# Two transformer blocks on one core: other banks for three folded norms, a shorter wait before their first passes, and edits at the head and in the convolution's tail

## Time and profile before

| | us |
|---|---|
| median of 3 runs | 1256.05 (1254.77 to 1258.88) |
| the profiled execution's own time | 1254.8 |
| its span in the trace | 1253.1 |
| PE busy in the span | 1216.1 (97%) |
| the chain that ended last, on PE | 80% |
| bytes read from HBM | 352.58 MB, 282 GB/s over the span |

### The profile page before, as it was taken

The page is one execution under the profiler, slowest core; times in us unless marked ns, Lnnn a source line. Parts: engine busy times, 40 slices in busy tenths (PEclk is TensorE's granted clock), DMA queues, the critical chain, the costliest instruction groups (busy, mean ns, idle before and its releaser), DMA issues.

```text
span 1253.1 us, 16148 instructions
## 1 busy us (share of the span) xinstructions
PE 1216.1 (97%) x6246; PEld 821.3 (66%) x6246; DVE 721.4 (58%) x1337; ACT 519.4 (41%) x903; POOL 48.1 (4%) x96
## 2 busy tenths in 40 slices
PE   9999999999999999999999999999999999999996
PEld 8997888887777778888877976634444334443332
DVE  5786877777758778777778988522222222222222
ACT  5554444444567654444456435422232222232222
POOL 0000000000000000000002800000000000000000
PEclk9999999999999999999999999999999999999998
DMA  8558777651631397766614486999999999999995
GB/s 294 198 217 298 269 269 268 246 190 68 228 135 31 110 364 268 269 252 239 229 57 147 149 277 261 358 421 404 427 428 431 427 429 429 428 427 431 428 426 206
DMA packets 121564, 358.07 MB, mean 286 GB/s; under 512 B 8890, under 2 KB 67955, under 8 KB 105106
## 3 DMA queue, kind: packets, MB, share of 16 engines
q1 hardware_dynamic: 114912, 331.85, 68.4%
q0 software_dynamic: 6336, 25.17, 5.1%
q10 hardware_dynamic: 242, 0.06, 0.0%
HBM read 352.58 MB, written 1.05 MB: 282 GB/s over the span
## 4 chain that ended last, share of the span: by engine, by line
PE 80%; DVE 7%; DMA 7%; ACT 3%; issue 1%; ACTq 0%; SPq 0%; DVEq 0%
PE ps L444 15%; PE ps L446 15%; PE ps L445 15%; PE ps L3084 14%; PE ps L3122 7%; DMA third_gate_up<-in_moe_w_up 5%; DMA second_expert<-in_moe_w_up 2%; DVE w_lo L418 2%; PE ps L3060 2%; PE ps L2503 1%; DVE xn L2600 1%; PE ps L3138 1%; PE ps L3067 1%; PE ps L3141 1%; PE ps L1039 1%
## 5 line engine op out<-in xcount | busy, mean ns | idle before, releaser
L413 ACT CAST w_hi<-dense_weights 128x1024 fp32r<-128x1024 f32 (+1 forms) x228 | 235.4, 1042 | 234.0 <-PE ps L446 194.5
L418 DVE TENSOR_TENSOR w_lo<-dense_weights,w_hi 128x1024 fp32r<-128x1024 f32 (+1 forms) x228 | 273.3, 1210 | 84.2 <-ACT w_hi L413 83.5
L444 PE MATMUL ps<-w_hi,xT_lo 128*128 128x512 f32 (+1 forms) x596 | 235.7, 395 | 4.4 <-DVE xT_lo L941 2.0
L446 PE MATMUL ps<-w_hi,xT_hi 128*128 128x512 f32 (+1 forms) x596 | 230.7, 387 | 0.0
L445 PE MATMUL ps<-w_lo,xT_hi 128*128 128x512 f32 (+1 forms) x596 | 230.3, 386 | 0.0
L444 PEld LDWEIGHTS ps<-w_hi,xT_lo 128*128 128x128 f32 x596 | 112.0, 188 | 32.0 <-issue 4.1
L446 PEld LDWEIGHTS ps<-w_hi,xT_hi 128*128 128x128 f32 x596 | 112.0, 188 | 23.3
L445 PEld LDWEIGHTS ps<-w_lo,xT_hi 128*128 128x128 f32 x596 | 112.1, 188 | 21.9 <-issue 0.2
L3268 DVE SCALAR_TENSOR_TENSOR cmask<-g_v,ps 128x256 f32<-128x256 f32 x32 | 13.5, 421 | 167.1 <-ACT g_v L3197 167.1
L3259 DVE TENSOR_TENSOR hnT<-ps,g_bc 128x512 f32<-128x512 f32 x32 | 22.1, 692 | 149.2 <-PE ps L3122 149.2
L3197 ACT ACTIVATE g_v<-ps 128x256 f32<-128x256 f32 x32 | 12.3, 384 | 206.7 <-PE ps L3084 206.7
(11 more groups left out here) (441 smaller groups left out, 1844.4 us busy)
## 6 DMA issues: line engine op xcount, KB each, us to landing
ada_w<-in_ada_w POOLq DMA_DIRECT2D x12, 2048.0 KB, 12.1
dense_weights<-in_w_gate SPq DMA_DIRECT2D x22, 1024.0 KB, 7.1
dense_weights<-in_w_up SPq DMA_DIRECT2D x22, 1024.0 KB, 9.4
dense_weights<-in_w_down SPq DMA_DIRECT2D x22, 1024.0 KB, 5.1
dense_weights<-in_moe_w_gate SPq DMA_DIRECT2D x10, 2048.0 KB, 21.6
second_expert<-in_moe_w_gate SPq DMA_DIRECT2D x9, 2048.0 KB, 20.4
second_expert<-in_moe_w_up SPq DMA_DIRECT2D x9, 2048.0 KB, 24.8
third_gate_up<-in_moe_w_up SPq DMA_DIRECT2D x9, 2048.0 KB, 27.2
```

The costliest lines, as they stand in the source:

```text
L413: act.copy(split_view(w_hi, name, i, j), piece(name, i, j)).then_inc(hi_ready, 1)
L418: dve.tensor_tensor(split_view(w_lo, name, i, j), piece(name, i, j), split_view(w_hi, name, i, j).bitcast(F32), ALU.subtract).then_inc(pie ...
L444: pe.matmul(out, left[1], right[0], start=start, stop=False)
L446: return pe.matmul(out, left[0], right[0], start=False, stop=stop)
```

## The change

1. **Norms.** Norms 1, 3 and 4 turn their chunks in banks 6, 7, 2, 3, in 4, 6, 5, 7 and in 4, 5, 2, 3. All folded norms do group 2 token tile by token tile. PE then waits for two finished chunks (four still in norms 2 and 5), and the piece loops behind norms 1, 3 and 4 wait for two more chunks before each piece.
2. **Head.** ACT issues one row load (`g_mix`), loads its table by a tiny activation, and issues the other 11 row loads later, behind the weight splits of the first block. The columns of `g_mix` are copied before the first split. The first 1 MB of weights comes in two DMAs; the warm-up counts are 12 and 14 for 24 and 6; the other columns of `cols_a` get a PE transpose and an ACT copy of their own in `pe_rest` and `act_rest`; `load_late` goes behind the loads of `ev_w_out`; the `dw_rows` load is cut in two. In the first piece PE waits for one high half, then for the second.
3. **Tail of the convolution.** `feature_cols` is copied by DVE, behind the first weighing; the weighing reads the gate from PSUM; the low part of the first block's last piece is made before the centring; the second block's first piece is split by ACT ahead of `act_rows`, which copies three banks for four.
4. **Experts' loads.** The gate half of expert 0 is issued after the taps on PE, expert 1's gate and up in four pairs of slices as the pieces of the second block are used, expert 2's up in two parts between them.

The diff, cut to its core (counts of landings that follow from it are left out):

```diff
@@ tokens_by_columns
-                    pe.wait_ge(*high)
-                    for part in range(2):
-                        for kk in range(2):
+                    for kk in range(2):
+                        pe.wait_ge(high[0], high[1] + kk * high[2])
+                        for part in range(2):
@@ columns (SP)
-                        sp.dma_start(dst[:, 0:4], wv[:, 0:4, c:c + n]).then_inc(gu_landed[0], 16)
+                        for piece_ in range(2):
+                            cut = slice(2 * piece_, 2 * piece_ + 2)
+                            sp.dma_start(dst[:, cut], wv[:, cut, c:c + n]).then_inc(gu_landed[piece_], 16)
...
-                    elif name == "ev_in" and i == 2:
-                        setup.load_late(sp)
@@ SP, behind the loads of ev_out
+            setup.load_late(sp)
@@ SP, experts
+            def feature_pair(e, k):
+                cut = slice(k, k + 2)
+                for side in range(2):
+                    sp.dma_start(gate_up_of(e)[:, side, cut], (g, u)[side][:, e, cut]).then_inc(gu_landed[e % TILES], 16)
...
             side_features(2, 0, 0, small_landed)
+            wait_split("conv_out", 0, 3, None)
+            gate_or_up(0, 0)
...
-            wait_split("conv_out", 0, 3, None)
-            gate_or_up(0, 0)
-            wait_split("conv_out", 1, 3, None)
-            side_features(0, 1, 1, gu_landed[0])
-            down_half(0, 0, down_landed[0])
+            for j in range(4):
+                if j == 1:
+                    wait_split("conv_out", 1, 3, None)
+                    side_features(0, 1, 1, gu_landed[0])
+                    down_half(0, 0, down_landed[0])
+                wait_used(sp, "conv_out", 1, j)
+                feature_pair(1, 2 * (PIECE_AT["conv_out", 1, j] % BUFFERS))
+                if j % 2 == 1:
+                    split_features(2, 1, j // 2)
             sp.wait_ge(h_ready, 28)
-            gate_up(1)
-            gate_or_up(2, 1)
@@ NormStage
-                banks = {0: (4, 5, 6, 7), 2: (4, 6, 5, 7), 5: (4, 6, 5, 7)}.get(self.index, (0, 1, 2, 3))
+                banks = {0: (4, 5, 6, 7), 1: (6, 7, 2, 3), 2: (4, 6, 5, 7), 3: (4, 6, 5, 7), 4: (4, 5, 2, 3),
+                         5: (4, 6, 5, 7)}.get(self.index, (0, 1, 2, 3))
...
-                    if self.folded and b % 2 == 0 and (self.index, b) != (3, 2):
-                        pe.wait_ge(h_ready, 4 * self.index - 2 + 2 * (b // 2))
-                    tiles_first = (self.index, b) == (3, 2)
+                    if self.folded and b == 0:
+                        pe.wait_ge(h_ready, 4 * self.index - 2)
+                    tiles_first = self.folded and b == 2
...
-                    pe.wait_ge(self.ready, KC * self.index + KC // 2)
+                    self.wait_chunk(pe, KC // 2 - 1 if self.index in (2, 5) else 1)
@@ FfnStage.pe
-                        if n == 0 and j == 2:
-                            self.norm.wait_rest(pe)
+                        if n == 0 and j >= 1:
+                            self.norm.wait_chunk(pe, 2 * j + 1)
@@ SetupStage
+            def load_table(self, act):
+                act.wait_ge(self.own_consts, 3)
+                act.activation(rtmp[:, 0, 0:1], ones[:, 0:1], ACT.Square)
...
-                warm_up(pe, 3, 24)
+                warm_up(pe, 3, 12)
                 pe.wait_ge(self.consts, 1)
-                pe.wait_ge(self.rows_landed, 16 * len(ROWS_A))
...
+                pe.wait_ge(gu_landed[2], 16)
...
-                warm_up(pe, 3, 6)
+                warm_up(pe, 3, 14)
@@ pe_rest
+                pe.wait_ge(self.rows_landed, 16 * (len(ROWS_A) - 1))
+                pe.transpose(ps[:, 6, ROWS_A_AT:ROWS_A_AT + N_ROWS_A], rows_a[0:N_ROWS_A, :], ident[0:N_ROWS_A, 0:N_ROWS_A])
@@ EvenStage.act
                 split_upto(act, split_hi, "ev_in", 0, 3)
+                setup.load_rows(act)
                 wait_used(act, "ev_in", 0, 3)
@@ OddIn.pe
-                        rest = lambda: self.norm.wait_rest(pe)
...
+                                      chunks=(self.norm.ready, KC * self.norm.index + 2, 2) if i == 0 else None)
@@ ConformerStage.act
-                mod.act_eights(act)
...
                 high(KC - 1)
+                split_upto(act, split_hi, "conv_out", 1, 0, ahead=0)
                 mod.act_rows(act)
@@ ConformerStage.dve
+                split_upto(dve, split_lo, "conv_out", 0, 3, ahead=0)
                 dve.wait_ge(self.conv, KC - len(CONV_PE))
...
+                    if c == 1:
+                        dve.wait_ge(mod.spread, 2)
+                        wait_a(dve, "conv_out", 1)
+                        weigh(0)
+                        mod.dve_eights(dve)
                     if 1 <= c <= KC:
                         finish(c - 1)
...
-                split_upto(dve, split_lo, "conv_out", 0, 3, ahead=0)
-                dve.wait_ge(mod.rows, 2)
-                wait_a(dve, "conv_out", 1)
```

More of the change, by code:

```diff
@@ L121 @@
 N_ROWS_A = sum(c for _, c in ROWS_A.values())
+FIRST_ROWS_A = ROWS_A["g_mix"][1]
 N_ROWS_B = sum(c for _, c in ROWS_B.values())
-SMALL_LANDED = 16 * (11 + len(ROWS_B))
-LATE_LANDED = 16 * 3
+ROWS_A_AT = 3 * P
+SMALL_LANDED = 16 * (12 + len(ROWS_B))
+LATE_LANDED = 16 * 4
 class Own:
@@ L532, in wait_gate_up @@
         def wait_gate_up(eng, e, it):
[L534 removed]
+            ahead = (16, LATE_LANDED + 96, 32)[e % TILES]
             eng.wait_ge(gu_landed[e % TILES], per_round(ahead + 32 * (e // TILES + 1), it, 32 * DOWN_TILES))
@@ L872, in act @@
                     if self.index == 0:
+                        gains(act)
                         split_upto(act, split_hi, *split_ahead, 0, ahead=0)
@@ L877, in act @@
                     act.activation(xn[:, 0], h[:, 0], ACT.Copy, scale=rstd[:, 0, 0:1]).then_inc(self.scaled, 1)
-                if gains is not None:
+                if gains is not None and self.index:
                     gains(act)
@@ L1267, in load_stream, with load_first_row @@
                     sp.dma_start(h[:, t], x[:, t]).then_inc(self.h_landed[t], 16)
+            def load_first_row(self, act):
+                for dst, src in list(self.rows(ROWS_A, rows_a))[:1]:
+                    act.dma_start(dst, src).then_inc(gu_landed[2], 16)
             def load_rows(self, act):
-                for dst, src in self.rows(ROWS_A, rows_a):
+                for dst, src in list(self.rows(ROWS_A, rows_a))[1:]:
                     act.dma_start(dst, src).then_inc(self.rows_landed, 16)
@@ L1396, in pe @@
                     tokens_by_columns(pe, "ev_in", i, (2 * i, 2 * i + 1), chunks=(norms[0].ready, 2, 2) if i == 0 else None,
-                                      high=(norms[0].hi, 2) if i == 0 else None)
+                                      high=(norms[0].hi, 1, 1) if i == 0 else None)
                 setup.pe_rest(pe)
@@ L1556, in pe @@
                         self.up.q_products(pe)
-                    tokens_by_columns(pe, "od_in", i, [2 * i + t for t in range(T)], width("od_in", i), rest, rest_at=3 if i == 2 else 2)
+                    tokens_by_columns(pe, "od_in", i, [2 * i + t for t in range(T)], width("od_in", i), rest, rest_at=3,
+                                      chunks=(self.norm.ready, KC * self.norm.index + 2, 2) if i == 0 else None)
             GATE_BANKS = (2, 5)
@@ L2285, in pe @@
                         tokens_by_columns(pe, "od_out", i, (4 + 2 * i, 5 + 2 * i), pieces=(2 * half, 2 * half + 1),
-                                          chunks=(self.lo, 3, 1) if late else None, high=(self.hi, 3) if late else None)
+                                          chunks=(self.lo, 3, 1) if late else None, high=(self.hi, 3, 0) if late else None)
                     if half == 0:
@@ L2394, in pe_eights, with dve_eights @@
                 last.then_inc(self.spread, 1)
-            def act_eights(self, act):
-                act.wait_ge(self.spread, 3)
-                act.copy(feature_cols[:], ps[:, 2, 0:2 * KC].rearrange("p (v k) -> p v k", v=2)).then_inc(self.rows, 1)
+            def dve_eights(self, dve):
+                dve.wait_ge(self.spread, 3)
+                dve.tensor_copy(feature_cols[:], ps[:, 2, 0:2 * KC].rearrange("p (v k) -> p v k", v=2)).then_inc(self.rows, 1)
             ROW_BANKS = (0, 1, 4, 5)
@@ L2410, in act_rows @@
                 act.wait_ge(self.spread, 2)
-                for i in range(2):
-                    bank = self.ROW_BANKS[2 * i]
-                    last = act.copy(g_bc[:, i].rearrange("p (j n) -> p j n", j=2), ps[:, bank:bank + 2, :])
-                last.then_inc(self.rows, 1)
+                act.copy(g_bc[:, 0, 0:512], ps[:, self.ROW_BANKS[0], :])
+                bank = self.ROW_BANKS[2]
+                act.copy(g_bc[:, 1].rearrange("p (j n) -> p j n", j=2), ps[:, bank:bank + 2, :]).then_inc(self.rows, 1)
         class ConformerStage:
@@ L2529, in pe @@
                     tokens_by_columns(pe, "conv_out", i, self.OUT_BANKS[i], chunks=(self.lo, 2, 2) if i == 0 else None,
```

(9 more changed lines are left out.)

33 lines of the change are left out of this document (18 added, 15 removed).

## The result

| | before | after |
|---|---|---|
| median | 1255.41 us (6 runs, 1254.31 to 1258.88) | 1246.89 us (6 runs, 1246.22 to 1251.70) |
| ratio, with its 95% interval | | 0.9933 [0.9915, 0.9951] |
| profiled execution's own time, span | 1254.8, 1253.1 | 1248.71, 1246.9 |

The change is faster by 0.7%.

The account below looks back on a forecast made before the run. PE was taken to set the pace up to 806 us, then the DMA engines by the experts' bytes. Head -0.95, norms -2.37, tail -1.93 and experts 0 made -5.25, from 1256.05 to 1250.8 us, range 1247.0 to 1254.8.

Parts of the forecast that it names:

- the head's term: Head: -0.95 us, from -1.5 for an earlier first transpose, +0.2 for one more transpose and +0.35 for a stall.
- The tail's term: Convolution's tail: -1.93 us, -0.88 from earlier tanh and -1.05 from the removed wait for `w_lo`; bounds -1.0 and -2.1.
- the base: Starting time from which the forecast subtracts its terms: 1256.05 us, the median of the runs before.
- The gain of -1.5: Head: PE's first transpose at 10.55 instead of 12.05 us; bounds -2.0 (PE at the rate of scaling) and +1.0.
- The stall of 0.35 at piece 7: Head: ACT's 11 late issues delay `gm_v` and `w_lo` of piece 7, so PE stalls +0.35 us (0 to 0.7).
- The extra transpose: Head: one more PE transpose of 121 rows, for the other columns, costs +0.2 us (0.1 to 0.3).
- Cover is that PE has no hole from 12.05 to 36.10: Head: reason for pricing the moved `load_late` at zero, ahead of weights that PE doesn't wait for.
- Norms, -2.37: Norms 1, 3 and 4: PE starts two chunks earlier, 3 x 0.79 us; bounds 0 and -3 x 1.0.
- The finer wait on high halves gives nothing: Convolution's tail: all chunks come 0.88 us earlier and so does the block's end; the finer wait adds zero.
- Experts and prefetch, 0: Experts' stream: 0 us, an unbroken stream replaced by a start-up of some 1.5 us; bounds -0.8 and +0.5.
- the same work: Routing, 787.7 to 804 us: work unchanged by the change, so no term in the sum.
- Rival 1: Routing: PE's half clock falls at another moment, about 1.0 us more gain, 1249.8 (1249.0 with experts' -0.8); chance 0.17.

Follow-up runs that it names:

- head alone: The kernel before with only the head's part of the change; 1252.64 us, ratio 0.9980.
- no prefetch: The changed kernel with SP's experts' loads back in the order of before; 1248.20 us, ratio 0.9945.
- the changed kernel's second: The changed kernel run again with nothing edited, six more runs and another trace; 1248.92 us, ratio 0.9942.
- late loads kept: The changed kernel with positions and routing weights issued where the kernel before had them, behind the third block of ev_in; 1247.53 us, ratio 0.9950.
- wide logits: The changed kernel with the first 14 of 16 logits products of each kind over 72 columns instead of 36; 1247.72 us, ratio 0.9938.
- tap rows split alone: The kernel before with nothing but the tap rows in two transfers (16 + 15); 1254.46 us, ratio 0.9990.
- tap rows whole: The changed kernel with the 31 tap rows loaded in one transfer again instead of 16 + 15; 1249.90 us, ratio 0.9956.
- the single-chunk kernel: The changed kernel with PE waiting for single chunks where it waits for pairs; 1245.02 us, ratio 0.9915.

## Why the forecast fell short, step by step

The step that failed is the head's term: -0.95 was forecast, about -2.2 was measured. It charged a stall that doesn't exist, and it left out the split of the tap rows. The tail's term was too small by another 0.4 to 0.5, and the base was 1.2 too high.

**Head, -0.95: too small by 1.3, by a cost that isn't there and by an omission.** The gain of -1.5 was nearly right. The first transpose lay at 12.05 to 12.16 in four traces of the old head; in six with the new one (the changed kernel's first, head alone, no prefetch, the changed kernel's second, late loads kept, wide logits), it lay at 9.90, 9.96, 10.82, 10.58, 10.13 and 10.93: -1.7 in the mean, -1.5 forecast. What spreads them is PE's clock at the start. The forecast took the first 24 passes at 1.2 GHz to 7.1; where they took 5.4 to 5.5 us, as in the variant without prefetch, it was 10.6 to 10.9, bound by the warm-up:

```profile
1.84 5.49 PE L489 MATMUL ps<-ones 128*128 128x128 f32 x24 [1.84 <-POOL ones L1326]
7.47 3.51 PE L489 MATMUL ps<-ones 128*128 128x128 f32 x28
10.82 0.60 PE L981 MATMUL ps<-ident,xn 128*128 128x128 f32 x4
```

Where they took 4.35 or 4.44, the clock had risen on the way, and scaling ended last, at or just past the forecast's bound of -2.0.

The stall of 0.35 at piece 7 doesn't exist. It rested on 11 issues that begin when ACT's split has ended. In the changed kernel they begin as the split begins, since the issues go out beside it, and `gm_v` follows the last at once; it is copied at 24.96, against 25.27 in the earlier trace rows, 1.8 later than the shift alone would have it, and not 2.8. The low half of piece 7 was made by 30.85 in the variant without prefetch, and PE came to it at 31.84:

```profile
20.32 1.06 ACT L415 CAST w_hi<-dense_weights 128x1024 fp32r<-128x1024 f32 x1 [1.66 <-PE ps L448]
20.33 0.34 ACTq L1296 DMA_DIRECT2D rows_a<-in_g_ffn  x1
24.62 0.30 ACTq L1296 DMA_DIRECT2D rows_a<-in_ev_w_conv  x1
24.96 1.01 ACT L1472 COPY gm_v<-ps 128x1024 f32<-128x1024 f32 x1 [3.59 <-issue]
```

The extra transpose costs some 0.13, 0.2 forecast: from the first transpose to norm 1 are 87.76 with the tap rows split alone, and 87.9 in the new heads. And the omission: in the old head PE's start on the third block hung on the landing delayed by the tap rows, just in time in the profiled run (landing 34.79, PE 38.78, no wait shown) and 0.5 or 0.8 us late in two others. From first transpose to norm 1 are 87.98, 88.52 and 88.81 in the old head and 87.87 to 87.97 in the new: another -0.54, with the extra transpose already paid. Without the split what was won ahead of 38.8 would have been lost there (tap rows whole: a wait of 1.57, and norm 1 at 100.43). "Cover is that PE has no hole from 12.05 to 36.10" looked only at where PE stood then and not at how much room was left. Measured, the head is -1.7 - 0.5 = -2.2.

**Norms, -2.37: right.** -2.2 in the changed kernel, -2.1 to -2.3 alone. PE was held by the second chunk and not by the transposes: it starts 0.36 after the last transpose of norm 1 has started, and 0.07 after it where it waits for one chunk only.

**Tail, -1.93: too small by 0.4.** -2.4 in the mean of eight traces with the new tail. In the first trace the second piece starts at 760.95, 766.36 before, which is -1.08 beside the shift of 4.33 that was there already (0.88 forecast); the rest is -1.26 (1.05 forecast). The mechanism is as written, ACT's tanh behind the scaling and no wait for `w_lo`. One reading was off: ahead of the second piece the kernel before had no hole to speak of (0.09 us); the 2.10 ahead of the first one were its hole. "The finer wait on high halves gives nothing" was right of that wait and wrong of the place: pairs of low halves held PE for 1.08, as the single-chunk kernel shows.

**Experts and prefetch, 0: right in the number, not in the reason.** The kernels without a clock fall late in the stream took 446.2 to 446.9, whichever order of loads they had. The two things that were to replace each other are the same start-up, paid in both orders.

**Routing, "the same work": right of the work.** Rival 1 is what the first trace shows (0.93, 1.0 forecast), but it comes and goes in any of the kernels.

**The base.** 1256.05 was the median of three runs; in the later comparisons the kernel before had 1254.76 (29 runs), 1255.32 (11) and 1254.90 (17). The parts as measured make -2.2 - 2.2 - 2.4 = -6.8, and the twelve runs' median is 7.0 under 1254.9. With the right base and the parts as measured the forecast would have been 1248.1, inside its own range; 1246.89 lies another 1.2 lower. The next six runs of the same kernel lay 2.0 higher, so most of that remainder is put down to the luck of six runs. Whether the clock or the chip made it isn't shown: of the first six only one was traced, and it wasn't among the four fastest.

## What to carry to other kernels

Before an edit is priced at zero because "no hole is seen", read how far ahead of its use each transfer lands there: a gain upstream of a landing that is just in time is lost at it, and the edit that moves the landing is the one that pays. Look at how a small load is spread, also one that nobody waits for: 31 rows delayed a large load behind them on the same queue, 16 and 15 rows didn't. And take one trace's clock falls as luck until a second trace of the same kernel has them in the same place.

## What was unexpected of the hardware

A load of 31 rows of 4 KB left one DMA engine of 16 busy alone (share 0.06 to 0.07, 25 GB/s), and a 2 MB load behind it landed 5 us later than with 16 + 15 rows. ACT's DMA issues went out while its preceding instruction was still running (20.33 beside a cast from 20.32 to 21.38). Thirty-two products, 28 of them over 72 columns, took the 3.66 us that they took over 36. After a pause of 2.17 us on PE the granted clock was 0.59 over the next 4 us; after a wait of 2.24 us in another trace it stayed at 1.00, and so it did after a pause of 0.68.
